# Moving three short transfers and one PSUM wait in a transformer kernel on one Trainium2 core

## The reference

```
h = rmsnorm(x) * (1 + scale) + shift
q, k, v, f, u = split(h @ w_in)              # 512, 512, 512, 8, 512 columns
mix = concat(forgetting_attention(q, k, v, log_sigmoid(f + b)), multiscale_pool(u)) @ w_out
x = x + gate * mix
x = x + gate_f * hierarchical_moe(modulate(rmsnorm(x)))   # 4 groups of 8 experts
```

```
a = square(relu(rmsnorm(h) @ w_ff1))         # 1024 -> 4096
out = rmsnorm(h + a @ w_ff2)                 # 4096 -> 1024
```

## Time and profile before

| what | value |
|---|---|
| median of 3 runs | 778.2 us (775.39, 778.2, 780.11) |
| profiled execution | 776.65 us |
| its span | 774.8 us |
| TensorE busy | 691.5 us, 89% of the span |
| VectorE busy | 357.5 us, 46% |
| ScalarE busy | 295.5 us, 38% |
| moved by DMA | 210.27 MB, 271 GB/s over the span |
| mean granted TensorE clock | 0.97 of full |

### The profile page before, as it was taken

How to read it: one execution, slowest core, us unless ns; L and a number is a source line. 1 busy time by engine, 2 the same in 40 slices (tenths; PEclk the granted TensorE clock), 3 DMA queues, 4 the chain that set the end, 5 groups by cost and what they waited for, 6 DMA issues and landing times.

```text
span 774.8 us, 13061 instructions
## 1 busy us (share of the span) xinstructions
PE 691.5 (89%) x5482; PEld 540.4 (70%) x5482; DVE 357.5 (46%) x571; ACT 295.5 (38%) x432; POOL 46.5 (6%) x84
## 2 busy tenths in 40 slices
PE   3899999899757667778999999999998999999996
PEld 3787778743323222224999989998888999999995
DVE  3568861521110100105946885436664645555543
ACT  4235430331111010005764544578254633444432
POOL 0000000000000000000083740000000000000000
PEclk9999999999999898889999999999999999999999
DMA  8999899999999999999745344323353355554001
GB/s 342 407 416 388 310 424 419 422 422 422 423 422 424 423 422 425 399 413 425 297 164 218 110 161 165 112 103 115 110 208 145 115 211 217 217 189 183 11 1 54
DMA packets 33038, 210.27 MB, mean 271 GB/s; under 512 B 4688, under 2 KB 5072, under 8 KB 8656
## 3 DMA queue, kind: packets, MB, share of 16 engines
q1 hardware_dynamic: 32976, 209.38, 67.7%
HBM read 208.32 MB, written 1.05 MB: 270 GB/s over the span
## 4 chain that ended last, share of the span: by engine, by line
PE 69%; DMA 19%; DVE 6%; ACT 3%; SPq 2%; issue 2%; DVEq 0%; ACTq 0%
PE psum L419 68%; DMA raw<-in_w_exp 16%; DMA raw<-in_w_ada_q 3%; SPq L466 1%; DVE wlo L512 1%; PE psum L427 1%; ACT whi L495 1%; SPq L474 0%; DVE XL L1962 0%; DVE XL L2356 0%; DVE X L2398 0%; DVE acc L534 0%; ACT G L1283 0%; ACT XT L2342 0%; ACT Sp L838 0%
## 5 line engine op out<-in xcount | busy, mean ns | idle before, releaser
L419 PE MATMUL psum<-XH,whi 128*128 128x256 f32 x736 | 210.6, 286 | 5.5 <-DVE XL L2356 3.1
L419 PE MATMUL psum<-XH,wlo 128*128 128x256 f32 x736 | 208.8, 284 | 0.0
L419 PE MATMUL psum<-XL,whi 128*128 128x256 f32 x736 | 208.3, 283 | 0.0
L512 DVE TENSOR_TENSOR wlo<-raw,whi 128x2048 fp32r<-128x2048 f32 (+1 forms) x88 | 169.0, 1958 | 48.5 <-ACT whi L495 48.5
L495 ACT ACTIVATE whi<-raw 128x2048 fp32r<-128x2048 f32 (+1 forms) x79 | 139.4, 1802 | 37.4 <-PE psum L419 22.4
L419 PEld LDWEIGHTS psum<-XH,whi 128*128 128x128 f32 x736 | 139.8, 190 | 8.6 <-DVE XL L2356 3.3
L419 PEld LDWEIGHTS psum<-XL,whi 128*128 128x128 f32 x736 | 139.4, 189 | 0.3
L419 PEld LDWEIGHTS psum<-XH,wlo 128*128 128x128 f32 x736 | 139.4, 189 | 0.0
L419 PE MATMUL psum<-raw,G 128*32 128x512 f32 x456 | 68.0, 685 | 20.1 <-DMA raw<-in_w_exp 19.9
L419 PEld LDWEIGHTS psum<-raw,G 128*32 128x32 f32 x456 | 17.8, 123 | 57.6 <-issue 56.7
L419 PE MATMUL psum<-raw,XT 128*32 128x512 f32 x248 | 37.1, 732 | 20.0 <-DMA raw<-in_w_exp 18.5
(11 more groups left out here) (350 smaller groups left out, 948.8 us busy)
## 6 DMA issues: line engine op xcount, KB each, us to landing
raw<-in_w_exp SPq DMA_DIRECT2D x85, 1024.0 KB, 22.9
raw<-in_w_ff SPq DMA_DIRECT2D x32, 1024.0 KB, 5.3
raw<-in_w_in SPq DMA_DIRECT2D x22, 1024.0 KB, 6.1
raw<-in_w_ada SPq DMA_DIRECT2D x16, 1024.0 KB, 11.7
raw<-in_w_in_t SPq DMA_DIRECT2D x8, 1024.0 KB, 19.4
X<-in_w_exp SPq DMA_DIRECT2D x5, 1024.0 KB, 25.1
raw<-in_w_ada_q SPq DMA_DIRECT2D x4, 1024.0 KB, 15.3
raw<-in_w_out_t SPq DMA_DIRECT2D x4, 1024.0 KB, 9.4
```

The lines of the kernel that those rows point to most:

```text
L419: return e.matmul(o, l, r, start=start, stop=stop, skip_group_check=True)
L512: e.tensor_tensor(wlo[j % NS][:, x], ring[slot[i]][:, x], whi[j % NS][:, x], ALU.subtract).then_inc(*steps_(("lo", j, x.start // 1024), *[ ...
```

## The change

Three edits. The sync engine issues `wf`, `bfg` and `cst` after piece 11 instead of after piece 4. VectorE handles quarter 2 ahead of its wait for `cst` and of `late` and `SEL`, instead of behind them. In the feed-forward layer the wait for the reads of banks 0 to 3 is placed after the first-layer sum of j = 1, ahead of the first `pe_ff2`, instead of ahead of the loop.

```diff
@@ sp_mixer
             sp_small(e, "g", gcol[:, :, :], a["g_cols"])
-            sp_load(e, 5)
+            sp_load(e, 12)
             sp_small(e, "wf", wf[:, :, :], a["w_f"])
             sp_small(e, "bfg", bfg[:, :], a["b_fgate"][0:1, :].broadcast_to([128, 8]))
             sp_small(e, "cst", cst[:, NFIRST:NSOON], a["consts"][:, NFIRST:NSOON])
@@ dve_mixer
             dve_quarter(e, 1)
+            dve_quarter(e, 2)
             e.wait_ge(*loaded("cst"))
             e.tensor_scalar(late[:, 0:128], C["neg"][:, 128:256], -1.0, None, ALU.mult).then_inc(*mix_dve())
             e.tensor_scalar(late[:, 128:384], C["neg"], -1.0, None, ALU.mult).then_inc(*mix_dve("late"))
             e.tensor_copy(SEL[:, :], C["maskA"][0:16, :]).then_inc(*mix_dve("SEL"))
-            dve_quarter(e, 2)
             dve_pieces(e, 10)
@@ pe_ff
-            for k in range(4):
-                if k in holder:
-                    e.wait_ge(*at(("read", holder[k])))
             banks = Banks([4, 5, 6, 7])
             for j in range(9):
                 if j < 8:
                     feature_major(e, banks, fj(1, j), "n4", ff_pe, ("ff1", j))
+                if j == 1:
+                    for k in range(4):
+                        if k in holder:
+                            e.wait_ge(*at(("read", holder[k])))
                 if j:
                     pe_ff2(e, banks, j - 1)
```

## The result

| what | before | after |
|---|---|---|
| median of the timed runs | 777.51 us (4 runs, 775.39 to 780.11) | 771.37 us (4 runs, 770.89 to 771.94) |
| ratio | | 0.9916, 95% interval 0.9896 to 0.9937 |
| profiled execution | 776.65 us | 771.50 us |
| its span | 774.8 us | 769.7 us |

The change makes the kernel 0.84% faster by the ratio. The two medians are 6.1 us apart, the two profiled executions 5.15.

A forecast was written before the change was run, and what follows sets the result against it. The prediction took TensorE's mixer and feed-forward stretches as the bound, with DMA binding the expert stage between. It summed 0.95 + 2.1 + 1.4 = 4.45 us, 776.65 to 772.2, or 773.7 against the 778.2 median; range 771.0 to 777.3.

The forecast's parts named there:

- the 1.55 put back at the end: Whole kernel: the median lies 1.55 us above the profiled execution, added to the forecast after the sums.
- part 1: Mixer: moving the three transfers starts the q sum over chunks 6 and 7 earlier, worth 0.95 us, bounds 0 and 1.2.
- part 2: Feed-forward layer: with the wait moved, the first sum follows the first pair of low parts, worth 2.1 us.
- 1.4 of clock: Feed-forward layer: the granted clock no longer falls after the 3.1 us idle, worth 1.4 us, bounds 0 and 1.5.
- Rival (a): Feed-forward layer: the clock falls anyway; 775.2 us, chance 0.20.
- Rival (b): Mixer to experts: part 1 reaches nothing, some chain between 50 and 93 us does not hang on TensorE; 774.7 us, chance 0.13.
- The smaller price of bfg: Mixer transfers: the skill's 0.68 us for 4 KB, against the row's 1.88, would make part 1 worth about 2.1.
- Rival (c): Mixer: bfg is cheaper in its new place, piece 12's stretch and quarter 3's pinning come earlier; 772.5 us, chance 0.10.
- Within 0.5%: Whole kernel: the measured time differs from before by no more than 0.5%; chance 0.47.
- faster: Whole kernel: the change is faster by over 0.5%; chance 0.48.
- (d): Feed-forward layer: part 2 does nothing, the first sum meets its own equally late wait; 777.2 us, chance 0.04.
- (e): Mixer: slower, cst lands late with piece 14 and delays VectorE's queue and the q sum; 781.2 us, chance 0.03.

The follow-up runs named there:

- e1: Kernel before with only the feed-forward wait moved; 773.98 us against 776.82, ratio 0.9960.
- e9: Changed kernel timed again against the kernel before; 771.99 us against 777.72, ratio 0.9935.
- e3: Kernel before with only the three transfers moved behind piece 11, VectorE's order as before; 779.86 us against 776.82, ratio 1.0026.
- e4: Kernel before with only VectorE's order changed, quarter 2 ahead of the wait for cst; 776.90 us against 776.82, ratio 1.0002.
- e6: Changed kernel with the three transfers behind piece 13 instead of 11; 771.24 us, ratio 0.9917 to the kernel before (778.10).
- part 1 alone: Kernel before with only the transfers and VectorE's order changed, timed twice; 775.54 and 775.22 us, ratios 0.9980 and 0.9967.
- e8: Kernel before with only bfg issued later, behind psc; 775.85 us against 778.10, ratio 0.9974.
- the two filled ones: Kernel before with the feed-forward wait moved and extra matmuls in TensorE's waits for quarter 1; 774.49 and 774.26 us, ratios 0.9964 and 0.9951.
- e2: Kernel before with only the transfers and VectorE's order changed, feed-forward layer as before; 775.54 us against 776.82, ratio 0.9980.
- f1: Kernel before with only the feed-forward wait moved, timed again; 773.84 us against 778.23, ratio 0.9944.
- e5: Changed kernel with bfg issued behind psc instead of between wf and cst; 770.16 us, ratio 0.9910 to the kernel before (778.10).
- third comparison: Changed kernel timed once more against the kernel before, beside its two parts; 772.17 us against 778.23, ratio 0.9924.
- e7: Kernel before with the feed-forward wait ahead of the loop for two banks only, the others at j = 1; 774.54 us against 778.10, ratio 0.9958.
- e10: Kernel before timed against itself, unchanged; 777.02 us against 777.72, ratio 0.9998.

## Why the prediction was right or wrong

The forecast was 773.7 us, 4.45 us under a median of 778.2; measured were 771.37, and differences of 6.1, 5.7 and 6.1 us in three comparisons. The direction, the places and the order of the terms were right, the sum was about a quarter too small. Of the 2.3 us by which the time came out below 773.7, 1.6 belong to the 1.55 put back at the end, since the changed kernel's median lies just below its traced execution and not 1.55 above it; 0.7 belong to the sum, which gave 4.45 where the traces differ by 5.15. Of these 0.7, 0.2 are in part 1, 0.15 in part 2, and 0.3 between the two, where no term stood.

**Part 2, right.** 2.1 us of start and 1.4 of clock make 3.5; between the traces all that comes behind the last turning is 3.64 shorter (5.15 less 1.51), and 3.9 in e1 and e9. The first matmul is 2.56 earlier, where the prediction's own start gave 2.42, since TensorE follows the pair by 0.17 instead of 0.31; the four groups at VectorE's pace give 0.2 of it back. That leaves 1.3 for the clock, 1.4 taken. Rival (a) has fallen: eleven traces have an idle of 0.55 or 1.33 there, and no trace of them shows the clock under 1 from 580 to 620.

**Part 1, its way right, its size too small.** The failed step with the smaller share is "Part 1 is worth 0.95 us". Most links of the chain came as described: piece 9 at 33.0, cst at 40.6, VectorE's wait of 4.5, quarter 3 ready at 46.3 and pinned by piece 12 on ScalarE; e3, e4 and e6 show cst's and piece 12's parts one by one. One link failed: the waits for quarter 1 did not shrink to next to nothing. Piece 5 landed at 21.7 but piece 6 at 25.7, 4.0 us apart where other pieces lie 2.5 apart, and all nine traces with the transfers moved have one such step of 3.3 to 4.2 us among pieces 5 to 7 (in the trace of the kernel before one of 3.3 lies between pieces 8 and 9); why is open. It is not in the way at the end, since quarter 3 is pinned elsewhere. The sum over chunks 6 and 7 came at 46.35 and not at 46.7, 1.31 earlier than before, mostly because piece 12 was in 0.23 earlier; at the scores 1.17 of it were left. And 0.95 was read against a single execution, with 2.6 us of waits for quarter 1, where others of the same code had 2.6 to 3.5. The waits were taken as time that is given back in full at quarter 3. They have a second effect, which isn't given back: in part of the executions the clock falls behind them. In the traces 1.2 and, with the falls, 1.9 stand in place of 0.95; the timings of part 1 alone gave 1.3 and 3.0. That the falls are there is shown by two traces; how much of the median they make is not. Rival (b) has fallen as well: the 1.2 us pass through the experts' stream, and from the scores to the feed-forward layer's low parts fourteen of the traces lie between 513.9 and 514.6 us, before and after alike; e4 and e8, whose clock fell at 150 us, and the two filled ones take 515.4 to 516.7.

**The 1.55 put back, wrong.** The failed step with the larger share is "the 1.55 is put back at the end". I took the distance from the traced execution to the median, 776.65 to 778.2, as a constant of the measurement. The changed kernel's trace and median agree, 771.50 and 771.37, and its runs lie 0.8 to 2.7 us apart where those of the kernel before lie 4.6 to 6.4. So the distance belonged to the kernel before, whose traced execution lay below its median. Much of the scatter went with the change as a whole. What it was is open: the clock behind the two waits is one part in the traces, the feed-forward fall of 1.3 or 2.6 us another, and neither half of the change alone took the scatter away (e2 4.6 us in twelve runs, e1 2.9 in nine, f1 3.8 in six).

**The smaller price of bfg.** The 0.68 us that the Trainium skill (DMA: Bandwidth & Descriptors, Bandwidth) gives for 4 KB would have made part 1 2.1, near what was measured, but for a reason that isn't there: bfg cost 1.1 and not 0.68 in its new place, and piece 12 came 23.87 us after piece 4 instead of 23.69, not earlier. In the place between wf and cst the 0.68 disagrees with every trace. Rival (c) was right in its first half, bfg was cheaper in its new place, and has fallen in the second, since the stretch of piece 12 did not come earlier by it. What it described, bfg out of the way, is e5, and is worth 1.3 us at the scores.

**The chances.** "Within 0.5%" had 0.47 and "faster" 0.48; the measurement is clear of 0.5% in its whole interval in the first and third comparison. (d) and (e) did not occur; e3 shows what (e) would have looked like, one line away.

## What to carry to other kernels

Before a transfer is moved back, look at what stands behind its wait on each engine that uses it: the same move was 1.3 us better or 3 us worse by one line of VectorE's queue. A wait that is given back a few microseconds later can still be worth taking away, since TensorE can pay for its idle a second time, 1.3 to 2.6 us at 1.2 GHz: in every trace here behind an idle of about 3 us, and in two of six behind two waits of about 2 and 1.3 us. So a single trace of a kernel whose runs scatter by 5 us is one draw; take a second and a third before the difference to the median is added as a constant.

## What the runs showed of the hardware

- A transfer of 4 KB that repeats 8 floats over 128 partitions held the queue for 1.1 to 2.4 us behind wf (15 traces), in which a large piece moves 450 to 1000 KB at 2.47 us per 1024 KB, and for 0.2 to 0.8 us behind psc (3 traces). Issued behind psc, where nothing waited for it, it made the kernel before 2.2 us faster by itself (e8, ratio 0.9957 to 0.9990).
- The granted clock fell behind waits of 3.1 us (all seven traces with that wait), 2.95 us (e3) and, in two traces (e7, f1), behind two waits of 2.2 and 1.3, or 1.7 and 1.3 us, with 1.1 us of work between; in e10 it stayed full behind the same 1.7 and 1.3. In the feed-forward layer it stayed full behind 1.33 and 0.55. A fall cost about 1.3 us there in six traces and 2.6 in e3's, 1.4 in f1's mixer and 2.6 in e7's.
